# Moving GpSimd's weight splits around the cross-attention's softmax and around the sums of squares, in a two-layer encoder kernel

## The chip, the cores and the metric

The kernel runs on one core of a Trainium2 chip. The metric is the device time of one execution in microseconds (us). PE is TensorE, DVE is VectorE, ACT is ScalarE, POOL is GpSimd and SP is SyncE, whose queue here only starts transfers.

## What is computed

Two layers of a streaming encoder over 576 tokens: 512 of a prompt and 64 of a second request, which share the weights. A layer has four stages, each closed by a layer norm:

```python
x = layer_norm(ALPHA * x + 0.5 * swiglu(x, ffn1_gate, ffn1_up, ffn1_down), g[0], b[0])
mix, state = parallel_mixer(x, ...)      # 4 head groups, one input projection, W_out
x = layer_norm(ALPHA * x + mix, g[1], b[1])
x = layer_norm(ALPHA * x + cross_attention(x, mem_k, mem_v, w_q, w_o), g[2], b[2])
x = layer_norm(ALPHA * x + 0.5 * swiglu(x, ffn2_gate, ffn2_up, ffn2_down), g[3], b[3])

def cross_attention(x, mem_k, mem_v, w_q, w_o):
    q = (x @ w_q).reshape(B, T, 4, 64)
    s = einsum('bthd,bmhd->bhtm', q, mem_k) * 64 ** -0.5       # 256 memory tokens
    o = einsum('bhtm,bmhd->bthd', softmax(s), mem_v)
    return o.reshape(B, T, 256) @ w_o
```

The model width is 1024, the FFN width 2816; all is float32.

## The kernel before

**Products.** The big products run in fp32r as three passes: each operand is split into a rounded part (`hi`) and a rest (`lo`), and PE adds hi x hi, hi x lo and lo x hi. The activation lies transposed in `y`, `x_hi` and `x_lo` (128 x 8 blocks x 576 tokens), and is handled in two halves of 288 tokens. PE puts its results into four pairs of PSUM banks (`pairA`, `pairB`, `pairD0`, `pairD1`).

**Weight units.** All weights come as one stream of units of 128 x 1024 float32 (512 KB). A layer has 174. SP loads unit u into ring slot u mod 3 of `w_raw` as soon as unit u - 3 is split (L2619). POOL splits most of them in `unit` (L2479): one TENSOR_SCALAR copies 128 x 1024 rounded into `hi` (L2494) and four TENSOR_TENSOR of 128 x 256 subtract to make `lo` (L2501); before the first it waits for the load and for the slot being free. PE waits in `unit_there` for the count of split units, so the units are split in stream order. In the middle of an FFN other code, of seven products per pair of tiles, is used, in which ACT and DVE do part of the splitting (L2518 is POOL's part).

**Order.** Each engine's order is written out by hand, and engines meet at semaphores. POOL's list is at the end of its block, once per layer. `mix`, `cross`, `FFN2_AT` and `UNITS` are the numbers of the first unit of the mixer, of the cross-attention, of the second FFN and of the next layer. The first six units of each FFN and of the mixer are head units; PE reads them in `head`: for each half of the tokens first units 0 and 1 together as `x_ready` comes, with `stats` of the norm before in between, then units 2, 3, 4 and 5.

**Norms.** DVE adds the stage's result to `y` block by block (L1992) and sums the blocks of `y` into `scratch` (L2003; for the late halves POOL does so, L2555). ACT squares the blocks (L1349) into two scratch tiles in turn, and POOL adds the eight squares in seven adds in `squares_sum` (L2561); ACT's third square waits for POOL's first add. PE then means both sums over the partitions in `stats` (L757). From these DVE makes variance (L2010, L2011), centre (L2020), scale (L2027) and `x_lo` (L2031), ACT the root (L1354 to L1360), affine (L1366) and `x_hi` (L1371). In an FFN's tail the second half's products run on PE while the first half's norm is made: `stats` of half 0 stands between the tail's gate and up products of half 1, `stats` of half 1 in the next stage's head.

**The softmax of the cross-attention.** It has five blocks of rows (four of 128, one of 64), t = 0 to 4, with two blocks under way. DVE takes the minimum of the negated scores (L2446), ACT exponentiates and sums (L1682), DVE inverts the sum and scales the probabilities in four TENSOR_SCALAR of 128 x 256 (L2456), which counts `x.probs` up by one. PE turns the probabilities (L1116), makes the scores of block t + 2 (L1104) and multiplies with the values (L1132); ACT copies the turned ones (L1699). The last two blocks of queries come out of two bank halves that ACT reads at L1704, and PE turns block 0 into the same pair. Then follow ten matmuls whose result is not used (`keep_warm`, L614), the output product and the third norm.

Of the kernel before, what the change touches and what calls it, by code (L numbers as in the profile page):

```python
# [37 lines left out]
NCH = TP // CH  # L38
# [31 lines left out]
UNITS = 2 * FFN_UNITS + MIX_UNITS + X_UNITS  # L70
FFN2_AT = FFN_UNITS + MIX_UNITS + X_UNITS
# [3 lines left out]
HEAD, TAIL, HALF = 6, 6, 6  # L75
# [80 lines left out]
def build_program(nc, io, counts):  # L156
    made = {}
    with ExitStack() as ctx:
# [5 lines left out]
        def counted(name, pre=0):  # L164
            c = Count(sem(name), name, counts, pre)
            sem_list.append(c)
            return c
# [220 lines left out]
        def E(name):  # L388
            if name not in ev:
                ev[name] = counted(name)  # L390
            return ev[name]
# [773 lines left out]
        def freed_of(eng, l, label):  # L1165
            pair, n = uses[label]
            eng.wait_ge(pair.free.sem, pair.free.value(l, n + 1))
# [1312 lines left out]
        def _(pool):  # L2480
            made_hi = [0]
            for l in range(DEPTH):
                def unit(u, off=0):

                    w = u % UNITS
                    j = u % RING
                    raw_there(pool, l, u, off)
                    pool.wait_ge(unit_done, l * UNITS + (UNITS + BEFORE[w] + u - w + 1) + BODY * off)
                    if SLOT[w] in TAIL_SLOTS[2:]:
                        pool.wait_ge(product.sem, product.value(l, 7 * ((w // FFN2_AT + 1) * PAIRS - 1)  # L2490
                                                                + TAIL_OVER[w - w // FFN2_AT * FFN2_AT]))
                    hold(pool, "pool")
                    hi, lo = slots[SLOT[w]]
                    pool.tensor_scalar(hi, w_raw[:, j], 1.0, 0.0, ALU.mult, ALU.add).then_inc(unit_hi, 1)  # L2494
                    made_hi[0] += 1
                    pool.wait_ge(unit_hi, made_hi[0] + 4 * off)
                    for q in range(0, 8, 2):
                        b = slice(q, q + 2)
                        if (u == XQ1 + 1 or l == 0 and u in (2, 4)) and q == 6:
                            pool.wait_ge(unit_split, l * UNITS + u)  # L2500
                        i_ = pool.tensor_tensor(lo[:, b], w_raw[:, j, b], hi[:, b].bitcast(F32), ALU.subtract)  # L2501
                    i_.then_inc(unit_split, 1)
# [18 lines left out]
                def units(first, end):  # L2521
                    for u in range(first, end):
                        unit(u)

                def ffn_units(at):

                    fi = at // FFN2_AT

                    def half_body(k, off=0):
                        u = at + HEAD + HALF * k  # L2530
                        pair_lo(u, fi, 2 * k + 3, off)
                        unit(u + 2, off)
                        unit(u + 3, off)
                        pair_lo(u + 4, fi, 2 * k + 4, off)

                    half_body(0)
                    with pool.Fori(0, BODIES) as i:
                        half_body(1, i)
                        half_body(2, i)
                    made_hi[0] += 4 * (BODIES - 1)  # L2540
                    units(at + FFN_UNITS - TAIL, at + FFN_UNITS)

                def squares_sum(j, h, label=None):

                    c = slice(h * HT, h * HT + HT)
                    for n in range(1, KT):

                        if label:
                            if n == 1:
                                freed_of(pool, l, (label, h, 0))  # L2550
                            else:
                                pool.wait_ge(y_added.sem, y_added.value(l, (KT - 2) * (j - 1) + n - 1))
                            freed_of(pool, l, (label, h, n))
                            a = y[:, 0] if n == 1 else s1
                            pool.tensor_tensor(s1[:, c], a[:, c], y[:, n, c], ALU.add)\  # L2555
                                .then_inc((E("y_summed") if n == KT - 1 else y_added).sem, 1)
                        pool.wait_ge(sq_done.sem, sq_done.value(l, KT * (2 * j + h) + n + 1))
                        if n > 1:
                            pool.wait_ge(s2_added.sem, s2_added.value(l, (KT - 2) * (2 * j + h) + n - 1))
                        a = sil[0] if n == 1 else s2  # L2560
                        pool.tensor_tensor(s2[:, c], a[:, c], sil[n % 2][:, c], ALU.add)\  # L2561
                            .then_inc((stats_ready if n == KT - 1 else s2_added).sem, 1)
# [10 lines left out]
                mix, cross = FFN_UNITS, FFN_UNITS + MIX_UNITS  # L2573
# [1 line left out]
                    for u in range(0, HEAD, 2):  # L2575
                        unit(u)
                ffn_units(0)
                units(mix, mix + 2)
                squares_sum(0, 0)
                units(mix + 2, mix + 5)  # L2580
                squares_sum(0, 1)
                units(mix + 5, mix + HEAD)
                units(mix + HEAD, cross - 5)
# [3 lines left out]
                squares_sum(1, 1, ("mix", 3))  # L2587

                pool.wait_ge(h_ready.sem, l * h_ready.per + FFN_H + 8)
                units(cross + 3, FFN2_AT + HEAD)  # L2590
                squares_sum(2, 0)
                squares_sum(2, 1, ("cross", 0))

                pool.wait_ge(h_ready.sem, l * h_ready.per + FFN_H + 10)
                pool.wait_ge(stored["mk"], 16 * (l + 1))
                pool.wait_ge(stored["mvv"], 16 * (l + 1))
                ffn_units(FFN2_AT)
                last = l + 1 == DEPTH
                units(UNITS, UNITS + (0 if last else 2))
                squares_sum(3, 0)  # L2600
                units(UNITS + 2, UNITS + (2 if last else 5))
                squares_sum(3, 1)
                units(UNITS + 5, UNITS + (5 if last else HEAD))
            s2_added.n, stats_ready.n = 8 * (KT - 2), 8
# [251 lines left out]
```

## Time and profile before

| | |
|---|---|
| time, median of 3 runs | 2528.83 us (2525.9 to 2533.16) |
| the profiled execution's own time | 2531.46 us |
| its span | 2529.5 us |
| mean granted clock of PE in it | 0.978 |
| busy: PE, DVE, ACT, POOL | 95%, 68%, 36%, 56% |

All times inside the program are taken from the profiled execution, from the start of its span. In the answers of the trace "idle before" or a bracket tells how long an engine sat idle before an instruction and what released it. PEclk is the clock that TensorE was granted, 1.00 for 2.4 GHz and 0.50 for 1.2 GHz; in a stretch that has both it lies between.

### The profile page before, as it was taken

Reading aid. Unit: us, or ns where it says so; the run is one execution under the profiler, and the core shown is the slowest. Engines: PE = TensorE matmul, PEld = TensorE weight load, DVE = VectorE, ACT = ScalarE, POOL = GpSimd, SP = SyncE. Lnnn points to the kernel's source line nnn. Section 1 sums busy time; section 2 is a strip of 40 time slices with the busy share of each in tenths; the row PEclk is TensorE's granted clock in tenths of the full one; section 3 lists DMA queues with packets and bytes.
Section 4 is the critical chain, followed back from the end, with each engine's and each line's share of the span. In section 5 each row is a group of like instructions: output and inputs, shape, how many; then the busy total and the mean of one; then the engine's idle time right before and its main releaser. Section 6 shows DMA issues by size and latency. Waiting matters only on the chain. (4 is left out here: it accounts for less than half of the span.)

```text
span 2529.5 us, 49640 instructions
## 1 busy us (share of the span) xinstructions
PE 2398.0 (95%) x17586; PEld 2303.8 (91%) x17586; DVE 1720.9 (68%) x2569; ACT 922.0 (36%) x1760; POOL 1428.7 (56%) x1589
## 2 busy tenths in 40 slices
PE   7999999999988899999999999999999879999997
PEld 7999999988777799999999999999787768999997
DVE  6777765654557777777568777556546577877775
ACT  3333324332225633333343333244233256333324
POOL 4656666634249366566837556757342583756564
PEclk9999999989999999999999999999899989999999
DMA  5222222212112022222212222312121230222221
GB/s 187 95 89 99 83 100 74 73 54 76 63 51 95 26 80 96 76 99 100 92 47 101 87 80 100 102 56 84 51 94 37 69 102 1 101 91 91 85 91 55
DMA packets 61114, 204.10 MB, mean 81 GB/s; under 512 B 6808, under 2 KB 13976, under 8 KB 60312
## 3 DMA queue, kind: packets, MB, share of 16 engines
q1 hardware_dynamic: 52288, 184.83, 21.5%
q10 hardware_dynamic: 8664, 17.17, 1.9%
q8 instruction: 94, 1.54, 0.2%
q14 instruction: 68, 0.56, 0.1%
HBM read 195.66 MB, written 7.88 MB: 80 GB/s over the span
## 5 line engine op out<-in xcount | busy, mean ns | idle before, releaser
L2518 POOL TENSOR_TENSOR w<-w_raw,w 128x256 fp32r<-128x256 f32 x360 | 319.4, 912 | 306.3 <-DVE w_0f L1844 270.8
L2501 POOL TENSOR_TENSOR w<-w_raw,w 128x256 fp32r<-128x256 f32 x556 | 477.0, 888 | 11.6
L2494 POOL TENSOR_SCALAR w<-w_raw 128x1024 fp32r<-128x1024 f32 x139 | 150.3, 1081 | 307.9 <-issue 303.5
L494 PE MATMUL pairD<-h_hi,w 128*128 128x288 f32 x1536 | 279.5, 299 | 16.0 <-DVE kw L2264 6.3
L494 PEld LDWEIGHTS pairD<-h_hi,w 128*128 128x128 f32 x1536 | 231.6, 191 | 18.9 <-issue 8.4
L673 PE MATMUL pairB<-tq,w 128*128 128x288 f32 x1728 | 247.4, 295 | 0.0
L1910 DVE TENSOR_TENSOR y<-y,pairD 128x576 f32<-128x576 f32 x256 | 192.0, 750 | 75.4 <-PE pairD L494 73.7
L673 PEld LDWEIGHTS pairB<-tq,w 128*128 128x128 f32 x1728 | 235.9, 188 | 0.0
L2518 POOL TENSOR_TENSOR e<-w_raw,e 128x256 fp32r<-128x256 f32 x72 | 67.1, 953 | 254.9 <-ACT e L1253 254.9
L494 PE MATMUL pairD<-h_hi,d 128*128 128x288 f32 x1152 | 206.3, 295 | 1.2 <-DVE y L1910 1.2
L503 PE MATMUL pairD<-x_hi,w 128*128 128x288 f32 x832 | 174.7, 301 | 25.9 <-DVE w L1751 12.3
L673 PE MATMUL pairA<-x_hi,w 128*128 128x288 f32 x864 | 188.1, 294 | 0.0
L1870 DVE TENSOR_TENSOR scratch<-scratch,pairB 128x288 f32<-128x288 f32 x216 | 97.8, 453 | 122.9 <-PE pairB L673 120.2
L494 PEld LDWEIGHTS pairD<-h_hi,d 128*128 128x128 f32 x1152 | 171.0, 188 | 2.5 <-DVE y L1910 2.1
L494 PE MATMUL pairD<-h_lo,w 128*128 128x288 f32 x768 | 166.0, 298 | 0.0
L503 PEld LDWEIGHTS pairD<-x_hi,w 128*128 128x128 f32 x832 | 136.8, 191 | 29.8 <-issue 24.3
L1852 DVE TENSOR_TENSOR w<-w_0f,w 128x512 fp32r<-128x512 f32 x180 | 162.1, 900 | 0.5
L494 PE MATMUL pairA<-x_hi,w 128*128 128x288 f32 x832 | 157.4, 308 | 0.0
L2501 POOL TENSOR_TENSOR d<-w_raw,d 128x256 fp32r<-128x256 f32 x160 | 151.8, 978 | 3.3
L2561 POOL TENSOR_TENSOR scratch<-scratch 128x288 f32<-128x288 f32 x112 | 99.4, 887 | 85.4 <-ACT scratch L1349 79.3
L673 PEld LDWEIGHTS pairA<-x_hi,w 128*128 128x128 f32 x864 | 143.9, 188 | 0.0
L494 PEld LDWEIGHTS pairA<-x_hi,w 128*128 128x128 f32 x832 | 129.9, 197 | 2.4 <-issue 1.5
(413 smaller groups left out, 6249.3 us busy)
## 6 DMA issues: line engine op xcount, KB each, us to landing
w_raw<-in_stream SPq DMA_DIRECT2D x348, 512.0 KB, 3.5
out_ak<-pa ACTq DMA_DIRECT2D x2, 1152.0 KB, 4.1
out_y<-y SPq DMA_DIRECT2D x8, 288.0 KB, 2.2
mem_raw<-in_mem ACTq DMA_DIRECT2D x2, 1024.0 KB, 4.7
cst<-in_consts ACTq DMA_DIRECT2D x1, 1740.0 KB, 9.1
tb_dram<-in_rel ACTq DMA_DIRECT2D x2, 768.0 KB
y<-in_x ACTq DMA_DIRECT2D x2, 576.0 KB, 7.1
y<-in_x ACTq DMA_DIRECT2D x1, 1152.0 KB, 11.3
```

The source lines that it names most:

```text
L494: ins.append(mm(out[0:m, half, 0:n], wt, mv_[:, c:c + n], start=(start and i == 0), stop=(stop and i == 2)))
L503: return [mm(out[:, 0:HT], wt, mv_[:, c], start=(start and i == 0), stop=(stop and i == 2)) for i, (wt, mv_) in enumerate(((wh, hi), (wh, ...
L673: ins.append(mm(bank.t[:, 0:HT], wt[:, k], mv_[:, k], start=(start and k == i_ == 0), stop=(k == 3 and i_ == 2), skip_group_check=not start))
L1852: v.tensor_tensor(lo, raw, hi.bitcast(F32), ALU.subtract).then_inc(sum_lo.sem, 1)
L1870: v.tensor_tensor(out, a, b, op).then_inc(combined.sem, 1)
L1910: v.tensor_tensor(both(y[:, n]), both(y[:, n]), pair.halves(), ALU.add)\
L2494: pool.tensor_scalar(hi, w_raw[:, j], 1.0, 0.0, ALU.mult, ALU.add).then_inc(unit_hi, 1)
L2501: i_ = pool.tensor_tensor(lo[:, b], w_raw[:, j, b], hi[:, b].bitcast(F32), ALU.subtract)
L2518: i_ = pool.tensor_tensor(lo[:, c], src[:, c], hi[:, c].bitcast(F32), ALU.subtract)
L2561: pool.tensor_tensor(s2[:, c], a[:, c], sil[n % 2][:, c], ALU.add)\
```

## The change

On POOL's list two things are reordered, and one wait is new. In the tails of both FFNs one head unit of the next stage stands ahead of the first half's squares in place of two, and four in place of three ahead of the second half's. In the cross stage POOL splits the two units of `x_wo`, waits for the fifth `x.probs` of the layer, splits three of the six head units of the second FFN, adds both halves' squares, and splits the other three. The last layer's last tail has no units and is as before.

```diff
                 ffn_units(0)
-                units(mix, mix + 2)
+                units(mix, mix + 1)
                 squares_sum(0, 0)
-                units(mix + 2, mix + 5)
+                units(mix + 1, mix + 5)
                 squares_sum(0, 1)
...
                 pool.wait_ge(h_ready.sem, l * h_ready.per + FFN_H + 8)
-                units(cross + 3, FFN2_AT + HEAD)
+                units(cross + 3, FFN2_AT)
+                pool.wait_ge(E("x.probs").sem, E("x.probs").value(l, NCH + 1))
+                units(FFN2_AT, FFN2_AT + 3)
                 squares_sum(2, 0)
                 squares_sum(2, 1, ("cross", 0))
+                units(FFN2_AT + 3, FFN2_AT + HEAD)
...
                 last = l + 1 == DEPTH
-                units(UNITS, UNITS + (0 if last else 2))
+                units(UNITS, UNITS + (0 if last else 1))
                 squares_sum(3, 0)
-                units(UNITS + 2, UNITS + (2 if last else 5))
+                units(UNITS + 1, UNITS + (1 if last else 5))
                 squares_sum(3, 1)
```

POOL in the tail of the first FFN (a unit is a TENSOR_SCALAR and four TENSOR_TENSOR; L2561 are the adds of the squares), as the difference:

```order
 L2494 TENSOR_SCALAR w<-w_raw 128x1024
 L2501 TENSOR_TENSOR w<-w_raw,w 128x256 x4
-L2494 TENSOR_SCALAR w<-w_raw 128x1024
-L2501 TENSOR_TENSOR w<-w_raw,w 128x256 x4
-L2561 TENSOR_TENSOR scratch<-scratch 128x288 x7
+L2561 TENSOR_TENSOR scratch<-scratch 128x288 x7
+L2494 TENSOR_SCALAR w<-w_raw 128x1024
+L2501 TENSOR_TENSOR w<-w_raw,w 128x256 x4
 L2494 TENSOR_SCALAR w<-w_raw 128x1024
 L2501 TENSOR_TENSOR w<-w_raw,w 128x256 x4
```

One unit went from ahead of the seven adds to behind them. The same piece stands at the other two tails.

POOL behind the cross-attention, from the last head units on (ahead of these rows stand the units of `x_wo` and the first head units), as the two ends of the difference:

```order
 L2494 TENSOR_SCALAR w<-w_raw 128x1024
 L2501 TENSOR_TENSOR w<-w_raw,w 128x256 x4
-L2494 TENSOR_SCALAR w<-w_raw 128x1024
-L2501 TENSOR_TENSOR w<-w_raw,w 128x256 x4
-L2494 TENSOR_SCALAR w<-w_raw 128x1024
-L2501 TENSOR_TENSOR w<-w_raw,w 128x256 x4
-L2494 TENSOR_SCALAR w<-w_raw 128x1024
-L2501 TENSOR_TENSOR w<-w_raw,w 128x256 x4
 L2561 TENSOR_TENSOR scratch<-scratch 128x288 x7
 L2555 TENSOR_TENSOR scratch<-y 128x288
```

```order
 L2555 TENSOR_TENSOR scratch<-scratch,y 128x288
 L2561 TENSOR_TENSOR scratch<-scratch 128x288
+L2494 TENSOR_SCALAR w<-w_raw 128x1024
+L2501 TENSOR_TENSOR w<-w_raw,w 128x256 x4
+L2494 TENSOR_SCALAR w<-w_raw 128x1024
+L2501 TENSOR_TENSOR w<-w_raw,w 128x256 x4
+L2494 TENSOR_SCALAR w<-w_raw 128x1024
+L2501 TENSOR_TENSOR w<-w_raw,w 128x256 x4
 L2518 TENSOR_TENSOR e<-w_raw,e 128x256 x2
 L2518 TENSOR_TENSOR w<-w_raw,w 128x256 x4
```

Three units went from ahead of the squares of both halves to behind them. The instructions of PE, DVE and ACT stand in the same order as before.

## Rows read from the trace of the kernel before

**Rows 1.** The page, part 1: busy us, share of the span and instructions.
```profile
PE 2398.0 (95%) x17586; PEld 2303.8 (91%) x17586; DVE 1720.9 (68%) x2569; ACT 922.0 (36%) x1760; POOL 1428.7 (56%) x1589
```

**Rows 2.** Who PE waited for: us in total, times, longest us.
```profile
PE pairA L1116 <- DVE prx L2456: 18.2, 8, 3.4
PE pairD L503 <- DVE w L1751: 12.3, 1, 12.3
PE pairA L757 <- POOL scratch L2561: 10.5, 10, 2.5
```

**Rows 3.** Stretches of 20 us: first FFN's tail and softmax, first layer.
```profile
core 0: us, PE busy (x) PEld busy (x) DVE busy (x) ACT busy (x) POOL busy (x), PEclk, DMA share, GB/s
400.00:420.00 20.00, 18.68 (x124) 18.24 (x124) 15.44 (x26) 11.42 (x22) 15.23 (x19) 0.91 0.31 100
...
800.00:820.00 20.00, 14.86 (x99) 12.64 (x96) 14.21 (x19) 11.41 (x34) 19.42 (x24) 0.87 0.40 136
```

**Rows 4.** Timeline of DVE, softmax of layer 1: start, us, instruction, [idle before].
```profile
814.89 3.15 DVE L2456 TENSOR_SCALAR prx<-prx,small 128x256 f32<-128x256 f32 x4
...
823.50 2.55 DVE L2456 TENSOR_SCALAR prx<-prx,small 128x256 f32<-128x256 f32 x4
...
830.14 1.14 DVE L2456 TENSOR_SCALAR prx<-prx,small 128x256 f32<-128x256 f32 x4
...
832.09 1.13 DVE L2456 TENSOR_SCALAR prx<-prx,small 64x256 f32<-64x256 f32 x4
```

**Rows 5.** Timeline of DVE, softmax of layer 2.
```profile
2065.03 3.41 DVE L2456 TENSOR_SCALAR prx<-prx,small 128x256 f32<-128x256 f32 x4
...
2074.15 2.88 DVE L2456 TENSOR_SCALAR prx<-prx,small 128x256 f32<-128x256 f32 x4
```

**Rows 6.** Timeline of POOL, cross stage and third norm of layer 1.
```profile
800.95 1.67 POOL L2494 TENSOR_SCALAR w<-w_raw 128x1024 fp32r<-128x1024 f32 x1
...
845.34 0.80 POOL L2561 TENSOR_TENSOR scratch<-scratch 128x288 f32<-128x288 f32 x1 [18.70 <-ACT scratch L1349]
...
863.94 1.41 POOL L2561 TENSOR_TENSOR scratch<-scratch 128x288 f32<-128x288 f32 x1
893.45 2.43 POOL L2518 TENSOR_TENSOR e<-w_raw,e 128x256 fp32r<-128x256 f32 x2 [28.09 <-ACT e L1253]
```

**Rows 7.** Timeline of PE, the first turns and scores of both layers.
```profile
810.23 1.06 PE L1116 MATMUL pairA<-cst,prx 128*128 128x128 f32 x8 [2.49 <-DVE prx L2456]
811.22 2.08 PE L1104 MATMUL pairD<-mkT,qx 64*128 64x256 f32 x8
...
2061.32 1.06 PE L1116 MATMUL pairA<-cst,prx 128*128 128x128 f32 x8 [1.76 <-DVE prx L2456]
2062.31 1.13 PE L1104 MATMUL pairD<-mkT,qx 64*128 64x256 f32 x8
```

**Rows 8.** Timeline of ACT, its second read of the late queries, layer 1.
```profile
807.78 0.41 ACT L1704 ACTIVATE qx<-pairB 128x288 f32<-128x288 f32 x1
```

**Rows 9.** DVE's `x_lo` over the kernel (ns min/median/max), and PE behind the norm.
```profile
L2031 DVE TENSOR_TENSOR x_lo<-y,x_hi x64: 747/759/1650, 410.5 to 2527.7; 128x576 fp32r<-128x576 f32 x64
...
883.66 0.40 PE L503 MATMUL pairD<-x_hi,w 128*128 128x288 f32 x1 [1.22 <-DVE scratch L1795]
```

**Rows 10.** The chain that ended last, 24 matmuls at full clock: start, us.
```profile
2476.78 3.20 PE pairB L503 x24
```

**Rows 11.** Timeline of POOL, tail of the first FFN, layer 1.
```profile
388.20 1.05 POOL L2494 TENSOR_SCALAR w<-w_raw 128x1024 fp32r<-128x1024 f32 x1
...
413.01 0.81 POOL L2561 TENSOR_TENSOR scratch<-scratch 128x288 f32<-128x288 f32 x1 [0.29 <-ACT scratch L1349]
```

**Rows 12.** Timeline of PE, the same tail and the mixer's start.
```profile
400.30 0.75 PE L757 MATMUL pairA<-scratch,cst 128*128 128x288 f32 x2 [2.44 <-POOL scratch L2561]
...
420.58 0.37 PE L503 MATMUL pairD<-x_hi,w 128*128 128x288 f32 x1 [1.60 <-DVE y L1992]
```

**Rows 13.** Timeline of POOL, the last tail: first and last of seven adds.
```profile
2486.62 0.81 POOL L2561 TENSOR_TENSOR scratch<-scratch 128x288 f32<-128x288 f32 x1 [4.32 <-ACT scratch L1349]
...
2493.82 0.80 POOL L2561 TENSOR_TENSOR scratch<-scratch 128x288 f32<-128x288 f32 x1 [0.79 <-ACT scratch L1349]
```

**Rows 14.** Timeline of ACT, third square of half 1, first tail.
```profile
414.91 0.45 ACT L1349 ACTIVATE scratch<-y 128x288 f32<-128x288 f32 x1
```

## The prediction

> **What bounds the kernel now.** The page's first part [rows 1] has PE busy for 95% of a 2529.5 us span, so what a change can win is PE's idle time and the time in which PE runs at half clock. I then listed who PE waits for [rows 2]: the longest group is PE waiting for DVE's `prx` line, eight waits, 18.2 us in all; the third place is PE waiting for POOL's sums of squares, 10.5 us. Both are touched. The table of 20 us stretches [rows 3] says what such idle costs besides itself: PE is busy for 14.86 of 20 us in the softmax of the first layer, and its granted clock is 0.87 there; in the tail of the first FFN it is 0.91. The executed work around these places is the same before and after; only POOL's order and one wait change.
>
> **The softmax of the cross-attention.** Its five row blocks go round a loop: DVE scales the probabilities (four instructions, L2456), PE turns them (L1116) and makes the scores of the block after next (L1104), DVE takes their minimum, and scales the next block. PE waits for the scaling each time, so DVE's scaling is on the path. In the first layer the four instructions take 3.15 and 2.55 us for the second and third block and 1.14 for the fourth [rows 4]. What differs is POOL: it splits eight units in a row, the third of them from 800.95, and idles from 826.64 (845.34 less 18.70) [rows 6]; 830.14 is the first scaling after it. In the second layer the slow pairs are 3.41 and 2.88 [rows 5].
>
> Now POOL splits two units (they end at 800.95, before the first scaling) and then waits for the fifth `x.probs`, DVE's last scaling. All scalings run beside an idle POOL, so I price each at 1.14:
> - second and third block: (3.15 + 2.55) - 2 x 1.14 = 3.4 us in the first layer, (3.41 + 2.88) - 2.28 = 4.0 in the second;
> - first block: PE turned it at 810.23 after 2.49 us of idle [rows 7]. The scaling shrinks by 1.4 and what stands ahead of it too, but PE also needs the two banks that ACT empties until 807.78 + 0.41 = 808.2 [rows 8]. So PE starts at about 808.25: 2.0 gained, 0.5 of the idle left. In the second layer PE idled 1.76, and with the same 0.5 left 1.3 are gained.
> Sum: 5.4 + 5.3 = 10.7 us, all of it on PE's path.
>
> The clock: the scores that take 1.13 us at full clock (second layer) take 2.08 in the first, where the clock had fallen behind the 2.49 us of idle [rows 7]. With idle gaps of about 0.5 to 1.3 us in place of 2.5 the fall may stay away or come later. Bounds per layer: 0 and about three pieces of 0.95 = 2.9. I take 1.4, the middle, since gaps of 1.4 us remain: 2.8 in all.
>
> **What is behind POOL's new wait.** Three head units of the second FFN, then the squares of the third norm, then three more units. In the first layer the squares' first add was at 845.34, 18.7 us after POOL's last unit [rows 6]. From the end of the fifth scaling (832.09 + 1.13 = 833.2) [rows 4] to there are 12.1 us and three units at 3.9 to 4.2 each take 11.8 to 12.6: they just fit, and a start up to 0.5 late is made up, because POOL idled between the adds. Everything here moves earlier by the same gain, so the fit stays. Cost 0.
>
> The last three units follow the squares, which end at 865.35 (863.94 + 1.41) [rows 6]; at 3 x 4.2 to 4.4 they end 12.6 to 13.2 later, at 878.3 on the old time scale. PE needs the sixth one for the 24 matmuls that ended 1.22 before 883.66 [rows 9]; at 3.20 per 24 [rows 10] they start at 879.2. So it is in time by 0.9 us, the fifth by 2, the fourth by 3. SP may load the seventh and eighth unit's raw weights only when the fourth and fifth are split, now at about 869.7 and 874 where it was before 823; they are first used just ahead of POOL's row of 893.45 [rows 6], so a load has 19 us. Cost 0.
>
> What isn't free is DVE. It now does the second half of the norm beside a busy POOL. Its four `x_lo` subtractions (L2031) there ran with POOL at rest; over the kernel this instruction takes 0.76 in the median and up to 1.65 [rows 9], the long ones in stretches where POOL splits (the 1.65 in the second layer's softmax). PE did wait 1.22 us for the end of this DVE chain at 883.66 [rows 9], so a delay goes into the time. Bounds per layer: 0 and 4 x 0.9 = 3.6. I take 1.2 (a third: DVE waits 0.6 and 1.1 for ACT inside the chain, which hides some): 2.4 in all.
>
> Here a rule speaks against the change. The Trainium skill ("SBUF — State Buffer", Who interferes with whom) says that VectorE and GpSimd share one port pair under an exclusive lock: whichever starts first holds it for the whole instruction, and this holds for a VectorE instruction with two inputs in SBUF as for one in a fast two-port mode. The 1.14 against 2.55 agrees with it; by the same rule each `x_lo` could lose a whole POOL instruction, the upper bound above, and the sum would be 4.8 us worse. The shown `x_lo` of 1.65 is such a case.
>
> **The tails** (first FFN of both layers, second FFN of the first; the last tail has no units and isn't changed). One unit less stands ahead of the first half's squares. Before, POOL split a unit from 388.20 on [rows 11], did its seven adds only then, up to 400.17, and PE idled 2.44 us for them, to 400.30 [rows 12]; the clock fell behind that gap [rows 3]. The kernel's last tail shows the adds without a unit ahead: 2486.62 to 2494.62, 8.0 us [rows 13], paced by DVE. So the adds now run from 388.6 to 396.6, 3.5 earlier, and PE's 2.44 us and its clock dip behind it go away. But then POOL has four units in place of three ahead of the second half's adds. Three took 12.6 us (400.17 to 413.01 less 0.29 of idle), so four take 16.8: the adds of half 1 start at 413.4, where they started at 413.01 [rows 11]. ACT's third square needs the first of them, so it comes at 414.3 against 414.91 [rows 14], and by way of ACT's affine and DVE's last adds of half 1 it sets PE's start in the next stage, 5.7 later in both: about 420.0 against 420.58 [rows 12]. PE is now 3.6 us ahead, then idles about 4 to 5, and the clock likely falls there (it fell behind 2.44), which costs 1.6. Net per tail between -1.0 and +1.0: I take 0 for the two FFN 1 tails. In the tail of the second FFN POOL paced the end already, and the same count gives +0.4. **The gap moves, it doesn't go.** Bounds for the three together: -4 (adds early, clock held: 2.44 less half of it given back, per tail) and +3.
>
> **Sum.** -10.7 (scalings) - 2.8 (clock) + 2.4 (DVE beside the late units) + 0.4 (tails) = -10.7 us. The profiled execution took 2531.46 (span 2529.5), so it would be 2520.8; it lies 2.6 above the median of the runs, 2528.83, and by that the median becomes **2518.1**.
>
> **Rivals.**
> 1. *The clock holds and a tail pays.* The full 2.9 per layer comes back (3.0 more than I count), and the tails give 4.4 more than I count, their bound of -4: 2518.1 - 3.0 - 4.4 = 2510.7. For it: the last tail has no gap and no dip. Against: half 1's adds don't start earlier. Chance 0.15.
> 2. *The late units cost what they could.* Each `x_lo` of the norm's second half loses 0.9: 2518.1 + 4.8 = 2522.9. For it: the 1.65 row; against: the median of `x_lo` is 0.76 although POOL is busy for 56% of the span [rows 1]. Chance 0.17.
> 3. *The scaling isn't the pace.* If ACT's exponentials or PE's own chain are right behind the scaling, only the first blocks' 3.3 stays, and the give-back of 2.4 and the tails' 0.4 with it: 2528.3. Against: ACT's exponentials end some 3 us ahead of the scaling that needs them. It also stands for a wait that doesn't do what it says. Chance 0.08.
> 4. *Slower: POOL becomes late for the FFN head.* If the softmax gains nothing (its slow scalings were due to something else than POOL), the squares end at 865.35 as before, the three units end with or after PE's need at 879.2, DVE loses 3.6 in `x_lo` and 0.9 in the first token sum, and POOL's lateness adds 0.2: 4.7 per layer; each tail pays a clock dip of 1.6: 9.4 + 4.8 = +14.2, 2543. It decides the sign once the softmax gains less than these 14.2, 7.1 per layer, and all the costs are real together. Against: 1.14 stands in both layers exactly where POOL rests. Chance 0.05.
>
> **How the numbers follow.** My forecast has 0.55, with +-4 for its own bounds. The range 2509 to 2527 takes in rivals 1 and 2 and leaves out 4, most of 3 and the ends. A measurement of this kernel can tell 0.3% (7.6 us) from no change, so faster means below 2521.2: 0.85 of the forecast, all of rival 1, a quarter of rival 2: 0.47 + 0.15 + 0.04 = 0.66. Slower by as much: 0.04 from rival 4. The rest, 0.30, is within.
>
> **What would show it.** All scalings at 1.14 us in both layers; POOL idle from its second unit of the cross stage to the fifth scaling; PE's waits for `prx` down from 18.2 to about 8 us; PE's wait of 2.44 for the squares in the tails gone, and a longer one in its place at the start of the next stage. Wrong would be: scalings of 2 us or more with POOL at rest; a PE wait for POOL's split at the head of the second FFN; `x_lo` of 1.3 and more throughout the norm's second half; a tail whose next stage starts over 1.5 us earlier.

## The result and the profile after

| | before | changed |
|---|---|---|
| median of the runs | 2528.26 us (2522.95 to 2533.37, 22 runs) | 2524.43 us (2515.56 to 2528.39, 22 runs) |
| ratio to before | 1 | 0.9981, 95% interval 0.9973 to 0.9989 |
| profiled execution, its span | 2531.46, 2529.5 us | 2526.07, 2524.1 us |
| PE busy, DVE busy, POOL busy | 2398.0, 1720.9, 1428.7 us | 2396.6, 1710.9, 1433.4 us |

The change gains 0.19% (4.8 us by the ratio, which is taken over all runs; 3.8 us by the medians). Both are under half of the forecast 10.7 and within the 0.3% that I had called no difference, though the interval of the ratio doesn't reach to 1; 2524.43 lies in the range of 2509 to 2527.

Who PE waited for in the changed kernel (us in total, times, longest), to be held against [rows 2]:

```profile
...
PE pairD L503 <- DVE y L1992: 10.7, 6, 4.4
PE pairA L1116 <- DVE prx L2456: 8.3, 8, 1.4
...
PE pairA L757 <- POOL scratch L2561: 5.4, 5, 3.0
...
PE pairB L757 <- POOL scratch L2561: 2.2, 2, 2.0
...
PE pairB L503 <- POOL w L2501: 1.5, 1, 1.5
```

The wait for `prx` fell from 18.2 to 8.3 us as forecast. New or grown are these: PE waits 10.7 us for `y` (3.5 before); it waits 3.0 us at a stretch for POOL's squares in the third norm, and 2.0 us at another in the tail of the second FFN (L757 into `pairB`; 0.8 there before); and 1.5 us for POOL's split of a head unit.

The softmax of layer 1 on DVE, whose rows answer to [rows 4]:

```profile
806.53 1.14 DVE L2456 TENSOR_SCALAR prx<-prx,small 128x256 f32<-128x256 f32 x4
811.90 1.14 DVE L2456 TENSOR_SCALAR prx<-prx,small 128x256 f32<-128x256 f32 x4
816.93 1.14 DVE L2456 TENSOR_SCALAR prx<-prx,small 128x256 f32<-128x256 f32 x4
822.16 1.14 DVE L2456 TENSOR_SCALAR prx<-prx,small 128x256 f32<-128x256 f32 x4
824.11 1.13 DVE L2456 TENSOR_SCALAR prx<-prx,small 64x256 f32<-64x256 f32 x4
```

All are at 1.14, and the fifth starts 8.0 us earlier than in [rows 4], from a stage that begins at the same time (the table below). Then POOL in the same stage, whose rows answer to [rows 6]:

```profile
825.46 1.05 POOL L2494 TENSOR_SCALAR w<-w_raw 128x1024 fp32r<-128x1024 f32 x1 [24.62 <-DVE prx L2456]
826.59 2.77 POOL L2501 TENSOR_TENSOR w<-w_raw,w 128x256 fp32r<-128x256 f32 x4
829.33 1.05 POOL L2494 TENSOR_SCALAR w<-w_raw 128x1024 fp32r<-128x1024 f32 x1
830.46 3.82 POOL L2501 TENSOR_TENSOR w<-w_raw,w 128x256 fp32r<-128x256 f32 x4
834.25 1.05 POOL L2494 TENSOR_SCALAR w<-w_raw 128x1024 fp32r<-128x1024 f32 x1
835.39 3.50 POOL L2501 TENSOR_TENSOR w<-w_raw,w 128x256 fp32r<-128x256 f32 x4
838.85 1.02 POOL L2561 TENSOR_TENSOR scratch<-scratch 128x288 f32<-128x288 f32 x1
```

And ACT, which makes the squares, and PE, which waits for their sum:

```profile
834.72 0.45 ACT L1349 ACTIVATE scratch<-y 128x288 f32<-128x288 f32 x1 [2.02 <-DVE y L1992]
835.44 0.45 ACT L1349 ACTIVATE scratch<-y 128x288 f32<-128x288 f32 x1 [0.28 <-DVE y L1992]
839.91 0.78 ACT L1349 ACTIVATE scratch<-y 128x288 f32<-128x288 f32 x2 [4.02 <-POOL scratch L2561]
```

```profile
846.06 1.33 PE L757 MATMUL pairA<-scratch,cst 128*128 128x288 f32 x2 [3.03 <-POOL scratch L2561]
...
880.50 0.40 PE L503 MATMUL pairD<-x_hi,w 128*128 128x288 f32 x1 [2.94 <-DVE scratch L1795]
```

The first pair of squares is there at 835.9 (835.44 + 0.45). POOL comes out of its third unit only at 838.85, 2.95 us later; ACT has two buffers for the squares (`sil[n % 2]`) and stands for 4.02 us; PE idles 3.03. The granted clock is low behind that idle. The stretches around it (us, busy times, granted clock, DMA share, GB/s):

```profile
844.00:846.00 2.00, 0.00 (x0) 0.00 (x0) 0.00 (x0) 1.11 (x3) 1.71 (x4) 0.76 0.00 0
846.00:850.00 4.00, 3.94 (x12) 3.37 (x13) 1.58 (x4) 1.80 (x5) 4.00 (x7) 0.50 0.00 0
850.00:852.00 2.00, 2.00 (x11) 2.00 (x10) 1.02 (x3) 0.67 (x2) 2.00 (x3) 0.53 0.00 0
```

0.50 is the lower level, 1.2 GHz. In the second layer the clock was low for the last product with the values and for the filler (the ten unused matmuls, L614) before the norm (0.83 on average from 2070 to 2090), `y` came later for it, and the three units fitted, with 0.46 us over; there it was the sixth unit that was late, by 1.49:

```profile
2090.96 0.80 POOL L2561 TENSOR_TENSOR scratch<-scratch 128x288 f32<-128x288 f32 x1 [0.46 <-ACT scratch L1349]
...
2119.77 1.63 POOL L2494 TENSOR_SCALAR w<-w_raw 128x1024 fp32r<-128x1024 f32 x1
2121.49 4.84 POOL L2501 TENSOR_TENSOR w<-w_raw,w 128x256 fp32r<-128x256 f32 x4
```

```profile
2126.39 0.41 PE L503 MATMUL pairB<-x_hi,w 128*128 128x288 f32 x1 [1.49 <-POOL w L2501]
2130.69 0.40 PE L503 MATMUL pairD<-x_hi,w 128*128 128x288 f32 x1 [0.87 <-DVE scratch L1795]
```

In the tail of the first FFN, PE no longer waits at 400 ([rows 12] had 2.44 there), but at the start of the next stage:

```profile
419.91 0.58 PE L503 MATMUL pairD<-x_hi,w 128*128 128x288 f32 x1 [4.36 <-DVE y L1992]
```

Behind that idle, too, the clock is at the lower level (columns as in the stretches above):

```profile
420.00:424.00 4.00, 4.00 (x17) 4.00 (x18) 2.35 (x5) 1.01 (x3) 3.34 (x5) 0.50 0.00 0
```

Over the whole program no clock was gained: the mean granted clock is 0.978 in the profiled execution before and 0.976 in that of the changed kernel, whose 22 runs have 0.978 on average (the kernel before has 0.979 to 0.980 in the runs taken beside the experiments). Their times go with it, from 2515.56 us at 0.983 to 2528.39 at 0.975.

**Where the time went.** I took the start of the same DVE instruction in both traces and subtracted: the lead (-) or lag (+) over the kernel before, in its one profiled execution. That execution was 3.2 us slower than the median of its runs, and e1's was the slowest of seven, 4.0 above its median, so the row of the ends isn't the row of the medians. "Statistics" is DVE's first step behind `stats` (L2010), and the late units are those behind the squares. The kernels e1 to e10 are those of the next section.

| place | before, us | changed | e1 | e6 | e4 | e10 | e9 | e8 |
|---|---|---|---|---|---|---|---|---|
| tail 1 (FFN 1, layer 1), statistics of half 1 | 425.49 | +1.3 | +1.5 | +1.5 | -0.7 | +0.4 | -3.5 | -3.1 |
| cross stage of layer 1, its start | 793.75 | -0.2 | -0.6 | -1.0 | -3.2 | -4.8 | -7.7 | -5.8 |
| first `y` add behind it | 843.60 | -9.4 | -9.8 | -4.3 | -9.7 | -11.1 | -7.7 | -13.1 |
| third norm, statistics of half 0 | 854.10 | -5.7 | -6.2 | -4.2 | -9.7 | -11.1 | -7.7 | -13.1 |
| behind the late units (L1824) | 885.11 | -3.2 | -3.6 | -2.8 | -8.3 | -9.6 | -7.6 | -12.4 |
| tail 2 (FFN 2), half 1 | 1268.59 | -2.3 | -2.6 | -1.9 | -7.5 | -9.7 | -6.8 | -12.6 |
| tail 3 (FFN 1, layer 2), half 1 | 1679.86 | -0.7 | -2.5 | -4.3 | -6.3 | -10.2 | -8.7 | -15.2 |
| cross stage of layer 2, its start | 2043.98 | +1.9 | +1.2 | -1.7 | -3.9 | -7.4 | -6.1 | -10.8 |
| first scores' minimum (L2446) | 2054.66 | +0.5 | -0.2 | -3.0 | -5.3 | -8.6 | -7.4 | -12.1 |
| first `y` add behind it | 2095.96 | -6.7 | -7.4 | -9.3 | -14.6 | -18.2 | -8.2 | -21.0 |
| behind the late units (L1824) | 2137.73 | -5.6 | -6.3 | -8.2 | -13.5 | -17.0 | -8.5 | -20.6 |
| end | 2527.68 | -5.4 | -6.1 | -8.0 | -13.4 | -16.9 | -8.4 | -19.6 |

In layer 1 the changed kernel gains 9.2 us to the first `y` add, gives 3.7 back by the statistics of half 0 (the wait and the low clock behind it), and 2.5 more by the end of the late units. It comes out 3.0 ahead, where I had counted 5.4 + 1.4 - 1.2 = 5.6. In the mixers, whose own work no kernel touches, the lead moves by up to 5 us either way, so a sum over a whole trace isn't a measurement; I read single stages here, and the runs for the rest.

What moves it there is the clock. In the second mixer (from tail 3 to the cross stage of layer 2) all the changed kernels of the table lose 2.4 to 4.4 us of their lead. The kernel before is busy on PE for 339.9 us of that stretch at a mean granted clock of 0.97; each of the seven others has the same 2480 matmuls within one, PE busy for 343.4 to 345.4 us, and 0.95. In the first mixer it is the other way round: 0.95 before, and 0.97 in e10 and e9, which gain 5.2 and 4.2 us there. It doesn't follow the edits: of the kernels outside the table e2 and e7, with the same tails as the changed kernel, have 0.97 in the second mixer and lose nothing there (e3 and e5 lose 0.5 and 2.4). Why the clock differs, with the same instructions, isn't shown.

### The profile page after: what moved, and what is told of

It reads as the page before. It is cut to its first block and busy times, and to the rows that moved or that the text cites. A ratio compares the mean times of both kernels' runs of the same rounds, so it can differ in the third digit from the quotient of the medians.

```text
span 2524.1 us, 49642 instructions
## 1 busy us (share of the span) xinstructions
PE 2396.6 (95%) x17586; PEld 2301.4 (91%) x17586; DVE 1710.9 (68%) x2569; ACT 922.3 (37%) x1760; POOL 1433.4 (57%) x1589
## 5 line engine op out<-in xcount | busy, mean ns | idle before, releaser
L503 PE MATMUL pairD<-x_hi,w 128*128 128x288 f32 x832 | 180.2, 308 | 31.1 <-DVE w L1751 12.5
L1277 ACT ACTIVATE scratch<-pairA 128x288 f32<-128x288 f32 x72 | 29.6, 410 | 267.5 <-PE pairA L673 267.3
```

Of the source, the lines that this page charges most:

```text
L503: return [mm(out[:, 0:HT], wt, mv_[:, c], start=(start and i == 0), stop=(stop and i == 2)) for i, (wt, mv_) in enumerate(((wh, hi), (wh, ...
L1277: f(sil[0][:, half(h)], src, ACT.Silu).then_inc(gate_on.sem, 1)
```

## The experiments

Each change is shown against the kernel before, unless said otherwise. Times are medians; behind them stands the ratio to before, taken over all runs, with its 95% interval. With 5 to 12 runs of each kernel the two differ by up to 2.6 us (e4: -10.3 by the medians, 0.9949 is -12.9), and the difference of two kernels is uncertain by 2.5 to 5 us.

**The two parts apart.** e1 has the change at the cross-attention alone:

```diff
-                units(cross + 3, FFN2_AT + HEAD)
+                units(cross + 3, FFN2_AT)
+                pool.wait_ge(E("x.probs").sem, E("x.probs").value(l, NCH + 1))
+                units(FFN2_AT, FFN2_AT + 3)
                 squares_sum(2, 0)
                 squares_sum(2, 1, ("cross", 0))
+                units(FFN2_AT + 3, FFN2_AT + HEAD)
```

> Only the cross-attention part of the change; the tails as before. Theory A (each part keeps its own worth to the end; the tails' part costs, it isn't free): the cross part gains the 3.9 and 5.6 us by which the changed kernel's events lead behind its two cross stages, so 2528.3 - 9.5 = about 2519 us, ratio near 0.996, and PE's 2.44 us waits for the squares stand in the tails again. Theory B (the tails are worth nothing either way and the cross part's lead is lost later, to whatever is next in the line): 2524 us, ratio 0.998, as the whole change. Theory C, the forecast's own (tails +0.4 in all): 2524, too.

Measured: 2521.43 against 2527.26, -5.8 us; ratio 0.9977 (0.9966 to 0.9988). Less than theory A's 9.5 and more than the whole change has. e1's trace shows the same wait, 3.03 us at 845.62.

e2 has the tails alone (`units(mix, mix + 1)`, `units(mix + 1, mix + 5)`, and the same with `UNITS`):

> Only the tails' part: one unit of weights ahead of each half's squares in place of two, the cross stage as before. Theory A: the three tails lose 1.2 to 2 us each at their end, the first one's loss is partly taken up before the layer is through, so +3 to +5 us, 2531 to 2533, ratio 1.001 to 1.002; in the FFN1 tails PE waits 4.4 us for y at the start of the next stage and shows clock 0.50 behind it. Theory B and C: within 1 us of before.

Measured: 2530.15 against 2527.26, +2.9 us; 1.0012 (1.0002 to 1.0022). The tails' part costs. The 2.9 isn't the 4 of a sum over my table, but both parts stand: -5.8 + 2.9 = -2.9, and the whole change has -3.8.

**How many units ahead of the squares.** e3 is e1 with two units ahead and four behind:

```diff
-                units(FFN2_AT, FFN2_AT + 3)
+                units(FFN2_AT, FFN2_AT + 2)
...
-                units(FFN2_AT + 3, FFN2_AT + HEAD)
+                units(FFN2_AT + 2, FFN2_AT + HEAD)
```

> As e1, but two units ahead of the cross stage's squares and four behind them. Theory A: in layer 1, where POOL was late, the squares start about 3.3 us earlier and PE's 3.03 us wait for them is gone with its low clock; a fourth late unit (4.5 us) goes in behind the squares, so the sixth ends 1 us later than in the changed kernel. In layer 2, where POOL had waited 0.46 us for the squares, nothing is gained in front and the sixth unit comes 4.5 us later, on which PE waited 1.49 already. Sum against e1: -1.5 in layer 1 (DVE beside the late units takes half of it), +4 in layer 2: 2521 us. Rival D (late units cost nothing that counts, being late in front is all): -3 in layer 1 and 0 in layer 2, 2516 us.

Measured: 2532.70 against 2527.26, +5.4; 1.0013 (1.0001 to 1.0025). Both theories are wrong by far, to the slow side (by the ratio +3.3 us). In front all is well: POOL idles 4.91 us ahead of the squares, and the lead of 9.9 at the first `y` add is all there at the statistics. Then PE in layer 1:

```profile
864.34 0.40 PE L503 MATMUL pairD<-x_hi,w 128*128 128x288 f32 x1 [1.00 <-POOL w L2501]
...
870.87 0.40 PE L503 MATMUL pairA<-x_hi,w 128*128 128x288 f32 x1 [3.10 <-POOL w L2501]
...
877.97 0.61 PE L503 MATMUL pairB<-x_hi,w 128*128 128x288 f32 x1 [3.68 <-POOL w L2501]
```

It waits for the fourth, fifth and sixth unit, 7.8 us together, and in layer 2 for the same three 1.01, 1.37 and 5.32, 7.7 us. POOL there, the end of the fifth unit and the whole sixth:

```profile
2119.44 3.71 POOL L2501 TENSOR_TENSOR w<-w_raw,w 128x256 fp32r<-128x256 f32 x4
2123.12 1.55 POOL L2494 TENSOR_SCALAR w<-w_raw 128x1024 fp32r<-128x1024 f32 x1
2124.76 7.15 POOL L2501 TENSOR_TENSOR w<-w_raw,w 128x256 fp32r<-128x256 f32 x4
```

The last unit takes 1.6 + 7.2 = 8.8 us, since DVE works on the token sums beside it, four instructions of 1.8 to 1.9 us (1.36 in the kernel before). The 4.4 us that I had counted for a late unit hold only ahead of these sums.

**When POOL starts again.** e4 is e1 with the wait for the fourth scaling, not the fifth (`value(l, NCH)`):

> As e1, but POOL waits for the fourth scaling of probabilities, not the fifth. Its three units start 2 us earlier and stretch the fifth scaling (1.13 us alone) to 2 to 3 us, as they did before. Theory A: where POOL was late (layer 1) 2 us less of PE's 3.03 us wait, given back by 1 to 1.5 us of fifth scaling in each layer: 2518 to 2520, no difference from e1 that can be told. Rival E (the fifth scaling's stretch hides behind the turn): 2 us better than e1 in layer 1.

Measured: 2516.93 against 2527.26, -10.3; 0.9949 (0.9936 to 0.9963), better than e1 by 4.5 us (7.1 by the ratios). Rival E is right in its mechanism, and its 2 us are too few; theory A is wrong. The rows of DVE and POOL:

```profile
821.07 2.89 DVE L2456 TENSOR_SCALAR prx<-prx,small 64x256 f32<-64x256 f32 x4
```

```profile
820.49 1.05 POOL L2494 TENSOR_SCALAR w<-w_raw 128x1024 fp32r<-128x1024 f32 x1 [22.68 <-DVE prx L2456]
...
835.64 0.80 POOL L2561 TENSOR_TENSOR scratch<-scratch 128x288 f32<-128x288 f32 x1 [2.45 <-ACT scratch L1349]
```

The fifth scaling stretches from 1.13 to 2.89, and the first `y` add comes as early as in e3, where it took 1.13: PE is busy with the fourth block and needs the fifth later. POOL now waits for the squares, not the squares for POOL. In layer 2, with the clock at 1.00 from 2040 to 2100, it waits 0.31.

But is it the later start, or the count of units behind it? e10 keeps the changed kernel's wait for the fifth scaling and splits one unit before the rest:

```diff
-                units(cross + 3, FFN2_AT + HEAD)
+                units(cross + 3, FFN2_AT + 1)
+                pool.wait_ge(E("x.probs").sem, E("x.probs").value(l, NCH + 1))
+                units(FFN2_AT + 1, FFN2_AT + 3)
                 squares_sum(2, 0)
                 squares_sum(2, 1, ("cross", 0))
+                units(FFN2_AT + 3, FFN2_AT + HEAD)
```

> The changed kernel's wait (for the fifth scaling) kept, the tails as before, but one head unit split before the rest and so only two between the wait and the squares, three behind. Theory A (what failed in the changed kernel is that three units, 13.4 us, don't fit into the 9.9 us between the fifth scaling and the first pair of squares): two units, 8.8 us, fit; PE's 3.03 us wait for the squares in layer 1 goes, though the wait stands where it stood; the sixth unit is late by 1.5 as in e4; 2517 us, as e4. Rival K (it is the place of the wait, after the fifth scaling rather than after the fourth, that made e1 slower than e4): 2521, as e1.

Measured: 2515.85 against 2526.50, -10.7; 0.9960 (0.9946 to 0.9974). Theory A: the wait stands where it stood, two units fit, and the gain is e4's by the medians. (Its 9.9 us reach to the first of the two squares that POOL's first add needs; to the second it is 10.65.) POOL in layer 1:

```profile
822.40 1.04 POOL L2494 TENSOR_SCALAR w<-w_raw 128x1024 fp32r<-128x1024 f32 x1 [20.75 <-DVE prx L2456]
...
834.27 0.80 POOL L2561 TENSOR_TENSOR scratch<-scratch 128x288 f32<-128x288 f32 x1 [3.58 <-ACT scratch L1349]
```

PE's wait at L757 is 0.38 in place of 3.03, and the lead of 11.1 at the `y` add is still 11.1 at the statistics, where the changed kernel lost 3.7.

**The rest for its own sake.** e6 has no wait, only the order: three head units at once, three behind the squares.

> No rest: three head units at once, through the softmax as before, then the squares, then the other three. It prices the late half alone, and asks how much of the gain needs the rest for its own sake. POOL is through its three units at about 814 in layer 1, in the first two blocks' time, so the third to fifth scaling run at 1.14 beside an idle POOL, where before they were slowed to 2.5 (second) and 1.14 (the rest). Theory A: half of the softmax gain of 8 us per layer stays (the scalings of the first block are the slow ones, those behind 814 fast): -3 to -4 a layer; 1.25 a layer given back behind the squares: 2527.3 - 4 to 5 = about 2523 us. Rival G (the gain comes from the clock, which needs every block on time, not from the scalings): 2527 to 2530.

Measured: 2522.55 against 2527.40, -4.9; 0.9978 (0.9966 to 0.9990). That is theory A's 2523. The first scaling takes 2.54, the others 1.14:

```profile
806.40 2.54 DVE L2456 TENSOR_SCALAR prx<-prx,small 128x256 f32<-128x256 f32 x4
813.49 1.14 DVE L2456 TENSOR_SCALAR prx<-prx,small 128x256 f32<-128x256 f32 x4
```

So three units fewer in the softmax, put behind the squares, are worth as much by themselves as with the changed kernel's wait (e1, -5.8). A rest that doesn't make POOL late adds 5.8 by the medians (e10, -10.7) and 4.5 by the ratios, which is no more than the uncertainty of that difference.

**The sixth unit.** e5 is e4 with one head unit before the rest, three ahead of the squares and two behind:

> As e4 (tails as before, POOL rests until the fourth scaling), but of the six head units one is split before the rest, in the 5.7 us between the end of the last cross unit (797.8) and the first scaling (803.5), three ahead of the squares, two behind. Theory A (the sixth unit's place in the queue behind the squares is what costs): PE's 1.51 us wait for the split of the sixth unit goes in both layers, and part of DVE's give-back with it; together 1.2 us a layer, so 2516.9 - 2.5 = about 2514.5 us. Rival F (the unit before the rest pushes the first reductions and the first scaling out by as much, since DVE shares the time with it): no better than e4, 2517.

Measured: 2516.24 against 2527.40, -11.2; 0.9961 (0.9946 to 0.9975). Not to be told from e4. PE's wait of 1.51 for the sixth unit is gone, but at 875.29 it waits 1.89 for DVE, where e4 had 0.88: two thirds of the gain went into the wait that the other had covered. That is rival F's number, not theory A's 2514.5. In layer 1 the first reduction (L2446) also lost 1.3 us of the lead, as rival F has it; in e8 and e10, which put the same unit there, it didn't.

**The tails again.** e7 is e4 with the tails of the changed kernel:

> e4 with the tails of the changed kernel (one unit ahead of each half's squares). It prices the tails' part a second time, on another base. By the two prices so far (2.9 us from e2 against the kernel before, about 1 us from the changed kernel against e1) 1 to 3 us slower than e4: 2518 to 2520. Forecast's own term: +0.4, so 2517.3. In both FFN1 tails PE waits 4.4 us for y behind the tail.

Measured: 2519.77 against 2527.40, -7.6; 0.9969 (0.9958 to 0.9979). That is 2.7 worse than e4. With e2 (2.9) and the changed kernel against e1 (2.0), three pairs give 2.0 to 2.9 for the tails' part by the medians; by the ratios they give 5.1, 3.0 and 1.0. Each is uncertain by 2.5 to 4.5 us. All three are on the slow side, which the granted clock bears out (mean over all runs: 0.9816 in e4 against 0.9792 in e7, 0.9789 in the kernel before against 0.9778 in e2, 0.9786 in e1 against 0.9781 in the changed kernel), but the size is known only to a few us.

e8 is e5 with other tails: in the two FFN 1 tails one unit ahead, three between the halves, two behind.

```diff
-                units(mix, mix + 2)
+                units(mix, mix + 1)
                 squares_sum(0, 0)
-                units(mix + 2, mix + 5)
+                units(mix + 1, mix + 4)
                 squares_sum(0, 1)
-                units(mix + 5, mix + HEAD)
+                units(mix + 4, mix + HEAD)
```

> e5 with, in the two FFN1 tails only, one unit ahead of the first half's squares, three between the halves and two behind (before: two, three, one; the change: one, four, one). Theory H (in the changed kernel it is the fourth unit between the halves that makes the second half's squares late, and with them ACT and y): both 2.44 us waits of PE in these tails go and no 4.4 us wait comes for them, 1.5 us or so a tail, 3 us in all: 2511 to 2512. Rival I (the next stage is paced by the data of the second half, whatever POOL does): the same as e5.

Measured: 2510.95 against 2527.40, -16.5; 0.9935 (0.9921 to 0.9949), the fastest kernel of this study, 5.3 better than e5, where theory H had 2511 to 2512. Its POOL begins the adds of half 1 at 409.90, the changed kernel's at 413.67, one unit later:

```profile
409.90 0.81 POOL L2561 TENSOR_TENSOR scratch<-scratch 128x288 f32<-128x288 f32 x1 [0.91 <-ACT scratch L1349]
```

PE behind the tail then waits 1.95 (at 417.46), not 4.36 (at 419.91). In the changed kernel ACT stood 3.28 us for that first add with the third square, and behind the square in its queue stood the norm's work on `y` of half 0, without which DVE makes no `x_lo` and no further `y`:

```profile
415.03 0.78 ACT L1349 ACTIVATE scratch<-y 128x288 f32<-128x288 f32 x2 [3.28 <-POOL scratch L2561]
415.71 1.13 ACT L1366 ACTIVATE y<-y,prm 128x288 f32<-128x288 f32 x2
416.87 0.68 ACT L1371 ACTIVATE x_hi<-y 128x576 fp32r<-128x576 f32 x1
```

e9 puts the same three edits into the kernel before, with nothing else:

> The kernel before with one change: in the two FFN1 tails one unit ahead of the first half's squares, three between the halves, two behind. Theory H (one unit fewer ahead is worth PE's 2.44 us wait, and costs nothing when the unit that it displaces goes behind the second half rather than between the halves): the ledger of e8 against e5 gives 3.4 us at the first tail and 2.7 at the second of the FFN1 tails, of which some is lost in between; -3 to -5, 2523 to 2524 us. Against it (rival J: e8's lead over e5 was the clock's luck, since e5 shows a 0.97 in a tail where e8 shows 1.00): within 1.5 us of before.

Measured: 2523.70 against 2526.50, -2.8; 0.9991 (0.9981 to 1.0002). The interval reaches to no change, and the size lies between theory H's (3 to 5) and rival J's (under 1.5). Its trace has both gaps of 2.44 gone and 1.94 behind the tail in both layers. I take it as likely a gain; alone it isn't shown.

## Why the prediction was wrong

**The step that failed** is the one on what is behind POOL's new wait: "they just fit, and a start up to 0.5 late is made up ... Everything here moves earlier by the same gain, so the fit stays. Cost 0." I compared the three units (11.8 to 12.6 us) with the 12.1 us of the kernel before. Both numbers moved. The units took 13.4: the first 3.9 beside an idle DVE, the second 4.9 beside DVE's `h_lo` (L2128, two of 128x576 from 830.85 on), the third 4.6 beside its `y` adds and sums (L1992, L2003). And the time to fill shrank from 12.1 to 10.65 us (825.24 to 835.9), because it holds PE's work at the clock of the moment: the filler before the norm, the same ten matmuls, took 4.38 us before and 2.69 in the changed kernel, which is more than the whole difference. Its rows, first before, then changed:

```profile
838.32 4.38 PE L614 MATMUL pairD<-cst 128*128 128x288 f32 x10 [0.55 <-ACT qx L1722]
```

```profile
830.34 2.69 PE L614 MATMUL pairD<-cst 128*128 128x288 f32 x10 [0.55 <-ACT qx L1722]
```

Gaining the clock was in my forecast; that it shortens this interval too was not. What it cost: in the changed kernel's own trace 3.7 us, the lead lost between the first `y` add and the statistics (3.0 of idle, the rest at the low clock). By the runs e10 and e4, in which POOL is in time, are 4.9 and 4.5 us further below before than e1 (4.3 and 7.1 by the ratios), each uncertain by about 4.4. Not all of that need be POOL's lateness. From the start of the cross stage to the late units e10 and e4 gain 1.8 and 2.1 us more than e1 in layer 1, where e1 is late, but also 2.1 more in layer 2, where e1's POOL is in time; there e1's clock is 0.83 from 2070 to 2090 and theirs is 1.00. Nor is it one lucky profile each: the mean granted clock of all runs is 0.979 in e1 and 0.982 in e4 and in e10. What holds the clock up in them in layer 2 isn't shown.

**The tails** are the second step that was mis-sized: +0.4 forecast, 2.0 to 2.9 measured by the medians (1.0 to 5.1 by the ratios). In the FFN 1 tails the mechanism was right to the letter ("the gap moves, it doesn't go": I said about 420.0 and a gap of 4 to 5, it is 419.91 and 4.36), and so was the clock's fall behind it, 0.50 from 420 to 424. I had set the gain at 2.44 plus the old dip; but in the tail of the second FFN, where PE's 2.54 for the squares of half 0 went, 2.02 for those of half 1 and 1.06 for `y` came, and the granted clock from 1230 to 1290 fell from 0.97 to 0.91. And the old dip isn't there in every execution: at the same tail with the same code the granted clock from 380 to 432 is 0.97 in the kernel before, 0.93 in e1, and 1.00 in e4.

Together: 10.7 forecast, less about 4.7 for POOL's lateness and the 1.6 to 2.5 by which the tails cost more than forecast, leaves 3.5 to 4.4, and the medians have 3.8. That it meets so well is luck: each price is uncertain by some 4 us, and other terms were off too. The trace has 5.4 of the 10.7. The 5.3 that it lacks are made of 3.7 for the lateness, 3.4 for the tails beyond their 0.4, 1.3 in the norms behind and 1.1 in the mixers, less 2.9 by which the softmax's clock gave more than forecast and 1.4 gained just ahead of the softmax of layer 2.

Point by point, the others:

- *Scalings, -10.7*: right. All at 1.14, PE's waits for `prx` 8.3 us (about 8 forecast), the first turn at 808.18 (808.25 forecast).
- *Clock, -2.8 within 0 to 5.8*: too small for the softmax. To the first `y` add the stage gained 9.2 us in layer 1, and 7.2 in layer 2 from the first minimum on, 3.8 and 1.9 above the scalings' share. The upper bound of 2.9 for a layer left out the work behind the softmax. Over the program it was given back (0.978 before, 0.976 changed): behind POOL's lateness, in the tails, and in the second mixer.
- *Late units in time, cost 0*: wrong by a little. The sixth was late by 1.49 in layer 2 (and by 1.51 and 1.47 in the two layers of e4), because the unit that runs beside DVE's token sums takes 6.5 us, not 4.4. I had named a PE wait for POOL's split at this head as a sign of being wrong, and it came.
- *DVE beside late units, +1.2 a layer*: 1.7 in layer 1 (the lead goes from 4.9 at the statistics of half 1 to 3.2), 1.2 in layer 2, the sixth unit's wait within it. The four `x_lo` of layer 1 take 1.22, 0.97, 1.34 and 1.26 where they took 0.76, and those of layer 2 take 1.23, 0.75, 0.91 and 0.83. By the rule of the Trainium skill ("SBUF — State Buffer", Who interferes with whom) each could have lost a whole POOL instruction; they lost 0.44 on average in layer 1 and 0.17 in layer 2, against the 0.9 of my bound.
- *Rivals*: none of the four is what happened. Against the third I had put that ACT's exponentials end some 3 us ahead of the scaling; in the kernel before they end 4.9 to 6.9 us ahead of it for the second to fourth block, 1.1 for the first and 0.3 for the fifth. Rival 2 gives nearly the measured time, but for another reason: `x_lo` wasn't 0.9 longer. Rival 4 named POOL's lateness at the FFN head; in e3 it came, +5.4, at full gain of the softmax, which I had thought to exclude it.

Left open: why the clock in the second mixer differs between kernels that have the same instructions there, and how often it falls in which place; each kernel has one profile. The runs without a profile show the mean clock alone.

## What to carry to other kernels

When work is made to wait for an event, compare what is queued behind the wait with the time from that event to its next deadline, and take both as they will be after the change: the gain that you forecast (here the clock) shortens that interval. A queue has two ends: of six units one too many between the event and the deadline cost about 5 us (e1 against e10), one too many behind cost 9 to 11 (e3 against e1), so split the work into what fits before the rest, between the rest and the deadline, and behind it. And where an engine's queue holds two streams (ACT's squares and its norm), a producer that is late for the one stops the other.

## What I had not expected of the hardware

- The same sixteen matmuls of the last product with the values took 1.58 us in layer 1 of the changed kernel and 2.87 in layer 2, and 2.88 in layer 1 of e4 and e10, in each case behind PE waits of 0.8 to 1.4 us only. Nearly equal gaps leave the clock at 2.4 GHz in one execution and at 1.2 in another:

```profile
825.64 1.58 PE L1132 MATMUL pairB<-ptx,mv 128*64 128x128 f32 x16 [1.19 <-ACT ptx L1699]
...
2077.96 2.87 PE L1132 MATMUL pairB<-ptx,mv 128*64 128x128 f32 x16 [1.19 <-ACT ptx L1699]
```

- DVE and POOL slow each other by very different factors: four scalings of 64 partitions 1.13 to 2.89, a DVE subtraction 0.76 to 1.34, POOL's four subtractions of a unit 2.77 beside an idle DVE, 3.82 beside DVE's `h_lo`, 3.50 beside its `y` adds and sums, and 4.84 to 7.15 beside the token sums.
